# Two transformer blocks on one core: when the modulation, the norms' sums, the last mixer's meta queries and the store run

## What is computed

```python
for l in range(2):                                  # first block
    mod = silu(c) @ w_ada[l] + b_ada[l]             # and the same of c_ctx; w_ada[l] is 1024 x 6144
    sh1, sc1, gt1, sh2, sc2, gt2 = split(mod, 6)
    hx = rms_norm(x, g_norm1[l]) * (1 + sc1) + sh1  # the context tokens likewise
    q, k, v = split(hx @ w_in[l])                   # mixers a, b, c: attention, two with rope,
    o = concat(mixer_a, mixer_b, mixer_c)           # q and k normed by head; context for l = 0 only
    x = x + gt1 * (o @ w_out[l])
    hx2 = rms_norm(x, g_norm2[l]) * (1 + sc2) + sh2
    x = x + gt2 * conv_ffn(hx2, w_up[l], conv, w_down[l])
for l in range(2):                                  # second block, h = 16 meta tokens and x
    h = h + 0.5 * rmsnorm(swiglu(rmsnorm(h, g), w_ffn1_gu, w_ffn1_down), g)
    h = h + rmsnorm(token_mixer(rmsnorm(h, g)), g)  # forgetting attention (fox) and gated linear attention
    h = h + 0.5 * rmsnorm(swiglu(rmsnorm(h, g), w_ffn2_gu, w_ffn2_down), g)
return h[:, meta:]                                  # so the meta tokens' own rows of the last layer are not read
```

## Time and profile before

| what | value |
|---|---|
| median of 3 runs | 2582.66 us (2581.03 to 2585.74) |
| the profiled execution | 2583.32 us, span 2581.5 us |
| TensorE matmul busy | 2417.3 us, 94% |
| VectorE busy | 1478.6 us, 57% |
| ScalarE busy | 1210.6 us, 47% |
| GpSimd busy | 115.8 us, 4% |
| mean granted TensorE clock | 0.957 |
| transfers | 355.32 MB, mean 138 GB/s |
| chain that ended last | TensorE 82%, VectorE 8%, ScalarE 4%, issue 3%, DMA 2% |

### The profile page before, as it was taken

How to read it: one execution, slowest core, us unless ns; L and a number is a source line. 1 busy time by engine, 2 the same in 40 slices (tenths; PEclk the granted TensorE clock), 3 DMA queues, 4 the chain that set the end, 5 groups by cost and what they waited for, 6 DMA issues and landing times.

```text
span 2581.5 us, 48676 instructions
## 1 busy us (share of the span) xinstructions
PE 2417.3 (94%) x18241; PEld 2168.0 (84%) x18241; DVE 1478.6 (57%) x2455; ACT 1210.6 (47%) x2095; POOL 115.8 (4%) x196
## 2 busy tenths in 40 slices
PE   6799997999999799899999999999999998999998
PEld 4578675777777587899999988989999997898998
DVE  2354645555532555687566575566656647656664
ACT  1264733333322646565444455554445445565553
POOL 0001410000000004000000000000000000000000
PEclk8599997999999899899999989999999998999999
DMA  7721022545433230355555532435555553344554
GB/s 278 242 87 58 2 84 77 160 158 162 154 98 101 79 99 1 116 178 174 168 188 169 159 114 96 143 131 188 170 162 171 170 172 117 107 136 145 187 185 122
DMA packets 100475, 355.32 MB, mean 138 GB/s; under 512 B 11136, under 2 KB 12832, under 8 KB 100352
## 3 DMA queue, kind: packets, MB, share of 16 engines
q1 hardware_dynamic: 91264, 321.23, 38.6%
q0 software_dynamic: 9088, 32.41, 4.1%
HBM read 352.55 MB, written 1.05 MB: 137 GB/s over the span
## 4 chain that ended last, share of the span: by engine, by line
PE 82%; DVE 8%; ACT 4%; issue 3%; DMA 2%; DVEq 0%; ACTq 0%; POOL 0%; SPq 0%; POOLq 0%
PE ps L668 22%; PE ps L669 22%; PE ps L670 22%; PE ps L805 2%; DMA ada_raw<-in_w_ada 2%; DVE wl L1603 2%; PE ps L818 2%; ACT wh L1160 2%; PE ps L791 2%; PE ps L731 1%; PE ps L685 1%; PE ps L689 1%; PE ps L686 1%; DVE nrstd L1622 1%; DVE nh L1679 1%
## 5 line engine op out<-in xcount | busy, mean ns | idle before, releaser
L1603 DVE TENSOR_TENSOR wl<-raw,wh 128x1024 fp32r<-128x1024 f32 x574 | 701.3, 1223 | 560.9 <-ACT wh L1160 557.4
L668 PE MATMUL ps<-hH,wh 128*128 128x272 f32 (+2 forms) x2960 | 936.5, 316 | 45.0 <-DVE hL L1688 21.1
L669 PE MATMUL ps<-hL,wh 128*128 128x272 f32 (+2 forms) x2960 | 914.5, 309 | 0.0
L670 PE MATMUL ps<-hH,wl 128*128 128x272 f32 (+2 forms) x2960 | 912.7, 308 | 0.0
L1160 ACT ACTIVATE wh<-raw 128x1024 fp32r<-128x1024 f32 x574 | 602.1, 1052 | 371.3 <-PE ps L670 347.0
L668 PEld LDWEIGHTS ps<-hH,wh 128*128 128x128 f32 x2960 | 565.8, 191 | 93.6 <-issue 38.8
L670 PEld LDWEIGHTS ps<-hH,wl 128*128 128x128 f32 x2960 | 565.8, 191 | 24.0
L669 PEld LDWEIGHTS ps<-hL,wh 128*128 128x128 f32 x2960 | 566.5, 191 | 22.3 <-issue 1.7
L668 PE MATMUL ps<-actH,wh 128*128 128x272 f32 (+2 forms) x1136 | 344.1, 303 | 2.6 <-DVE wl L1603 2.1
L670 PE MATMUL ps<-actH,wl 128*128 128x272 f32 (+2 forms) x1136 | 343.5, 302 | 0.0
L669 PE MATMUL ps<-actL,wh 128*128 128x272 f32 (+2 forms) x1136 | 342.9, 302 | 0.0
(11 more groups left out here) (293 smaller groups left out, 2852.0 us busy)
## 6 DMA issues: line engine op xcount, KB each, us to landing
raw<-in_w_ffn_gu SPq DMA_DIRECT2D x176, 512.0 KB, 3.5
raw<-in_w_mix SPq DMA_DIRECT2D x98, 512.0 KB, 3.5
raw<-in_w_up SPq DMA_DIRECT2D x88, 512.0 KB, 3.5
raw<-in_w_ffn_down SPq DMA_DIRECT2D x64, 512.0 KB, 3.6
ada_raw<-in_w_ada SPq DMA_DIRECT2D x48, 512.0 KB, 5.2
ada_next<-in_w_ada POOLq DMA_DIRECT2D x48, 512.0 KB, 4.0
raw<-in_w_out SPq DMA_DIRECT2D x32, 512.0 KB, 3.4
raw<-in_w_down SPq DMA_DIRECT2D x32, 512.0 KB, 3.5
```

The lines of the kernel that those rows point to most:

```text
L668: pe.matmul(out, a_h, b_h, start=start, stop=False)
L669: pe.matmul(out, a_h, b_l, start=False, stop=False)
L670: return pe.matmul(out, a_l, b_h, start=False, stop=stop)
L1603: dve.tensor_tensor(wl[:, slot, :], raw[:, slot, :], wh[:, slot, :].bitcast(F32), ALU.subtract).then_inc(l_split, 1)
```

## The change

It does these things.

- Layer 0's modulation is made in two parts. Chunks 0 to 15 (`ADA_FIRST`, shift and scale of the first norm) come in the opening, with the first three weight chunks (`EARLY`) loaded between chunks 11 and 12, and the norm's sum after chunk 11. Chunks 16 to 47 are loaded by GpSimd's queue through two slots and multiplied two at a time between the head and value tiles (`rest_ada`, 16 places), their rows copied by VectorE (`rest_rows`) into one buffer, with `mod` of these made just before the attention.
- The tables are loaded once 12 chunks are used, not after the norm.
- The four norms use squares in a ring of two and a running sum (`sq_added`), made in the stage before (`in_out`, `in_down`), a last square summed by TensorE itself, Ln and Exp as root, and `first_group` for the first three tiles. Of the heads' sums and rotations, those of the first tiles are made later (`SUMS`, `TURNS`).
- Layer 1's modulation has seven chunks in the output projection instead of four.
- The lambda terms of both layers are made once, in the opening.
- The last mixer has 8 attention steps, without the meta queries.
- The last norm works on pairs of tiles, and each pair is stored by a transfer of its own.

```diff
@@ SyncE
+            for j in range(ADA_FIRST):
+                if j >= ADA_RING:
+                    sp.wait_ge(ada_used, j - ADA_RING + 1)
+                if j == ADA_FIRST - 4:
+                    for c in range(EARLY):
+                        sp.wait_ge(l_split, c + 1)
+                        sp.dma_start(raw[:, c, :], io["w_qk"][0, KT + c]).then_inc(raw_loaded[c], 16)
+                sp.dma_start(ada_raw[:, j % ADA_RING, :], io["w_ada"][0, j]).then_inc(ada_loaded[j % ADA_RING], 16)
...
-            sp.wait_ge(x_ready, 4 * 8 + 6)
-            sp.dma_start(io["out"].rearrange("(k p) t -> p k t", p=P), xT[:, :, X0:T1]).then_inc(out_done, 16)
-            sp.wait_ge(out_done, 16)
+            for q in range(4):
+                sp.wait_ge(last_pair, q + 1)
+                sp.dma_start(out[:, 2 * q:2 * q + 2], xT[:, 2 * q:2 * q + 2, X0:T1]).then_inc(out_done, 16)
@@ GpSimd
-                pool.wait_ge(h_ready, 8 * (2 * l + 1))
+                if l == 0:
+                    pool.wait_ge(ada_used, ADA_FIRST - 4)
...
+                if l == 0:
+                    for j in range(ADA_FIRST, NADA):
+                        pool.wait_ge(ada_used, j - 3 if j < ADA_FIRST + 2 else j - 1)
+                        pool.dma_start(ada_raw[:, j % 2, :], io["w_ada"][0, j]).then_inc(ada_rest_loaded[j % 2], 16)
@@ TensorE
             def norm(n):
-                pe.wait_ge(sum_ready, n.idx + 1)
-                pe.matmul(ps[:, 5, 0:n.T], ones[:], n.nrstd[:, 0, 0:n.T], start=True, stop=True).then_inc(ss_ready, 1)
+                pe.wait_ge(sq_added, (KT - 2) * (n.idx + 1))
+                pe.matmul(ps[:, 5, 0:n.T], ones[:], n.nrstd[:, 0, 0:n.T], start=True, stop=False)
+                pe.wait_ge(sq_ready, 8 * n.idx + 8)
+                pe.matmul(ps[:, 5, 0:n.T], ones[:], n.nsq[:, 1, 0:n.T], start=False, stop=True).then_inc(ss_ready, 1)
...
+                def rest_ada(h):
...
+                    g = (ADA_FIRST + 2 * h) // 4
+                    if h % 2 == 0:
+                        pe.wait_ge(ada_row_ready, g)
+                        if h:
+                            turn_rows(7, g - 1, ada_rows)
+                    for j in ada_hook(h):
+                        pe.wait_ge(ada_rest_loaded[j % 2], 16 * (h + 1))
+                        ada_chunk(6, j % 4, ada_raw[:, j % 2, :], silu_first)
...
+                first_group(S[f"k{l}"], hh_ready, h_ready, 8 * split_before[n.idx], T=T1)
+                rest_ada(0)
+                for i in range(GROUP, N_HEADT):
...
+                    head_sums(SUMS[i][0])
+                    rest_ada(i - 2)
...
-                feature_major(S[f"up{l}"], tq, n=n, after=None if l else next_ada)
+                first_group(S[f"up{l}"], hh_ready, h_ready, 8 * split_before[n.idx], T=tq)
+                feature_major(S[f"up{l}"], tq, after=None if l else next_ada, skip=GROUP)
@@ ScalarE
-            def norm(n):
...
+            def square(n, k):
+                if k >= 2:
+                    act.wait_ge(sq_added, (KT - 2) * n.idx + max(1, k - 2))
+                act.activation(n.nsq[:, k % 2, 0:n.T], xT[:, k, T1 - n.T:T1], ACT.Square, scale=D ** -0.5).then_inc(sq_ready, 1)
@@ VectorE
             def norm(n, before_scale=None):
-                while summed.get(n.idx, 0) < KT - 1:
-                    add_square(n)
-                dve.wait_ge(root_ready, n.idx + 1)
-                link(dve.reciprocal(n.rstd, n.rstd))
                 if before_scale:
                     before_scale()
+                dve.wait_ge(root_ready, n.idx + 1)
@@ mixer
-                self.i, self.g, self.p, self.qt = i, FOX_STEPS * l + i, i // 3, i % 3
+                self.i, self.g, self.p, self.qt = i, 12 * l + i, i // FOX_PER[l], i % FOX_PER[l] + l
@@ end
-            transition(norms["post_ffn2", 1])
+            last_norm(norms["post_ffn2", 1])
```

More of the change, by code:

```diff
@@ L304, in build_program @@
         ada_loaded = [sem(f"ada_loaded{s}") for s in range(ADA_RING)]
+        ada_rest_loaded = [sem(f"ada_rest_loaded{s}") for s in range(2)]
         ada_next_loaded = sem("ada_next_loaded")
@@ L846, in _ @@
             last.then_inc(cols_psum, 1)
+            pe.wait_ge(lam_prod, 1)
             for l in range(2):
-                pe.wait_ge(lam_prod, l + 1)
-                pe.matmul(ps[:, 6, 0:2], ones[:], lam[:, 0:2], start=True, stop=True).then_inc(lam_sum, 1)
+                last = pe.matmul(ps[:, 6, 2 * l:2 * l + 2], ones[:], lam[:, l, 0:2], start=True, stop=True)
+            last.then_inc(lam_sum, 1)
+            for l in range(2):
                 tq = T1 if l == 0 else TX
@@ new lines, in rest_rows, with first_modulation @@
+                def rest_rows(h):
+                    if l == 0 and h % 2:
+                        ada_rows_of((ADA_FIRST + 2 * h) // 4, 6)
+                def first_modulation():
+                    modulation(0, ADA_FIRST if l == 0 else NADA, ADA_FIRST // 4 if l == 0 else ADA_GROUPS)
+                if l == 0:
+                    n = norms["n1", 0]
+                    dve.wait_ge(tables_loaded, 16)
+                    link(dve.tensor_reduce(ada_sel[:], ident[:].rearrange("p (j c) -> p c j", c=32)[:, 0:2, :], AX.X, ALU.add))
+                    ada_rows_of(0, 0)
+                    for _ in range(KT - 2):
+                        add_square(n)
+                    ada_rows_of(1, 1)
+                    ada_rows_of(2, 0)
+                    for c in range(AHEAD):
+                        split(Stage("", None, 0, 0, 0, 0), Step(0, c, RING), 0)
+                    ada_rows_of(3, 1)
@@ L2041, in _ @@
+                norm(norms["n1", l], before_scale=first_modulation)
                 tiles = head_tiles(l)
```

367 lines of the change are left out of this document (217 added, 150 removed).

## The result

The changed kernel takes 2514.64 us (median of 4 runs, 2513.44 to 2526.68) beside 2581.85 for the kernel before: a ratio of 0.975, 95% interval 0.9717 to 0.9783. The forecast was 2504 with a range of 2492 to 2522. The time is in the range, 10.6 above the forecast; the gain is 67 us and not 79. The profiled execution took 2513.86 us, its span is 2511.8; the one of before 2583.32 and 2581.5.

The account below looks back on a forecast made before the run. The prediction took the opening to be bound by transfers (48 w_ada chunks, 25 MB) and the body by TensorE. Its terms summed to -78.9 us from the profiled 2583.3, by the median 2503.8: 2504 us, range 2492 to 2522.

Parts of the forecast that it names:

- Opening to the norm: Opening: 16 instead of 48 w_ada chunks ahead of the norm, which starts at 50.6 instead of 101.74: -51.1 us.
- Three tiles run together: Layer 0's first projections: norm start to end of third tile takes 19.8 us instead of 32.3, TensorE setting the pace: -12.5.
- w_ada in the projections: Layer 0's projections: 32 chunks at 0.57 and 8 turns at 0.92 on TensorE, +25.6 us; small load waits +2.
- the 11.7 from which they decide: Rival, layer 0's projections: POOL's loads land at their worst, 12.9 us; +98, 2602 us; decides from about 11.7; chance 0.03.
- Catch-up: Layers 0 and 1: late square sums delay ScalarE, which in layer 1 must catch up: +2 and +3 us.
- n2 of layer 0: Norm before layer 0's up stage: third tile at 427.5 instead of 446.4: -18.9 us, 9.9 of it the start.
- n1 of layer 1: Norm before layer 1's heads: third tile at 863.0 instead of 878.5, less 0.46 for a head's sums: -15.0 us.
- n2 of layer 1: Norm before layer 1's up stage, 256 columns: third tile at 1075.8 instead of 1083.5: -7.8 us.
- Attention openings: Opening of each attention: a low half and a split leave VectorE's path: -1.2 us.
- Mixer: Mixer of layer 1: four meta-query steps go, each 0.26 for scores, 0.1 transposes, 0.22 values: -2.3 us.
- End: End: eight steps of 512 columns -0.35, and only the last 256 KB stored behind the last add, 2.3 less: -2.7 us.
- half restarts: Rival: restarts give half, ones-matmuls and first tiles at low clock, h's pace holding the group: +17, about 2521; chance 0.09.

Follow-up runs that it names:

- experiment 1: The changed kernel run again unedited, as yardstick on the same chip: 2519.45 us, ratio 0.9761 to the kernel before.
- experiment 10: Changed kernel with the head and bias tables issued when 16 w_ada chunks are used instead of 12: 2509.56 us, ratio 0.973 to the kernel before.
- experiment 4: Changed kernel with layer 1's head tiles run one by one instead of the first three together: 2516.44 us, ratio 0.9742 to the kernel before.
- experiment 3: Changed kernel with layer 1's up tiles run one by one instead of the first three together: 2516.59 us, ratio 0.9734 to the kernel before.
- experiment 5: Changed kernel with the four meta-query steps back in layer 1's mixer (12 steps, not 8): 2520.28 us, ratio 0.9752 to the kernel before.
- experiment 11: Changed kernel with one 1 MB store behind the last pair instead of four of 256 KB: 2523.16 us, ratio 0.9771 to the kernel before.
- experiment 6: Changed kernel with layer 0's head tiles run one by one instead of the first three together: 2519.91 us, ratio 0.9758 to the kernel before.
- experiment 7: Changed kernel with layer 0's up tiles run one by one instead of the first three together: 2515.62 us, ratio 0.9757 to the kernel before.
- experiment 8: Changed kernel with square root and reciprocal in the first block's four norms instead of Ln and Exp: 2530.27 us, ratio 0.9809 to the kernel before.

## Why the prediction came out right, and 10 us too good

Added up along the kernel by TensorE's own rows: at the end of layer 0's down stage it is 51.9 us ahead, where the terms make 53.5; at the end of layer 1's output stage 55.5, where they make 66.1; at the end 69.7 against 78.9. So most of what is missing arises in layer 1's heads and attention. Of that, the step of the prediction that failed is the catch-up behind the group, taken at 3 and measured at 6.2; the attention's part is chance. The row copy in layer 0's up stage cost 5.5, for which the sum had nothing, and was made good by an early opening and cheaper w_ada. All this is one trace: by experiment 1's medians (2519.45, still in the range) the forecast is 15 too good.

- **Opening to the norm: -51.1 forecast, -53.7 in the trace.** Held up: bytes at the measured rate set it (experiment 10). This execution was among the early ones: over the ten with this opening the norm starts at 50.2 in the mean, where the forecast had 50.6, and they spread over 5 us, for which it had no term.
- **"Three tiles run together": -12.5.** The 19.8 us from the norm to the third tile came out to the tenth in this trace; that is luck in part, since the other kernels with this group show 19.8 to 21.4. The reason was wrong. Without the group 4.7 of the 12.5 are lost. The rest goes with the norm's new order and the weight splits made ahead of it, read from the rows (first matmul 2.0 us behind the norm's start instead of 13.9) and tested by no run. After the catch-up, 0.2 to 3.4 us are the group's.
- **w_ada in the projections: +25.6, and +2 for loads.** Measured: pairs at 1.01 and turns at 0.88, 16 and 8 of them, 23.2, with no wait for a load at any of the 16 places; a chunk is 0.505 us and not the 0.57 of the earlier trace rows. The loads land in 4.5 us at the median, and but for the first pair, which has 34 us, 6.3 at most, far from the 11.7 from which they decide. The rule of the Trainium skill that was weighed there (SBUF — State Buffer, "SBUF: two separate sides") had no effect that these rows show; but no row tells whether VectorE ran anything in a two-port mode beside these loads, so it is not tested, here or in the earlier trace rows.
- **Catch-up: +2 and +3.** Layer 0: 1.84. Layer 1: this is the term that was mis-sized. The waits for sums and rotations are 9.0 us against 2.8 before, so 6.2, and 5.1 without the group (experiment 4). It was inside the bounds of 10 that the text gave, and taken at 3 although the text named the four heads and four copies that ScalarE has to make good.
- **n2 of layer 0: -18.9.** The start and the third tile came as forecast (18.3 by the tile behind the group). Then the row copy cost 5.5, so that the stage has -12.8. The text counted "a late copy of rows" (the 1.98 us at 429.19 above) among what this restart would get rid of, and gave no reason why the copy would come sooner. Behind a group VectorE has four evictions and a split to do at once, and TensorE waits for the copy that is queued behind them: 3.38 us and the low clock. "VectorE's idle half", by which the text calls other copies hidden, those of layer 0's late rows, is an average; these did stay hidden but for 0.8 us.
- **n1 of layer 1: -15.0.** To the third tile: 39.6 us before, 24.4 after, -15.3. Right, and then the catch-up took half: the heads went from 97.0 to 90.7.
- **n2 of layer 1: -7.8.** -9.2 at the third tile, but the stage ends with -4.9: the lead melts at 0.1 us a tile (experiment 3).
- **Attention openings: -1.2.** From the last value matmul to the first score it takes 2.8 us instead of 3.4 in layer 0, although the last w_ada pair and a turn now lie in it, and 2.55 instead of 3.2 in layer 1: -1.2, and the same within 0.03 us in the repeat. What lies behind is longer in this trace, from first score to output stage by 1.0 us in layer 0 and 2.8 in layer 1. In the other kernels, with the same code, it is 0.2 shorter to 1.5 longer and 0.2 shorter to 2.8 longer than before, so this part of the missing 10 us is chance.
- **Mixer: -2.3.** 1.04 a step, 4.2 in all (experiment 5). Its pieces were too low, 0.3 against 0.22 a step for the values, 0.2 against 0.1 for the transposes, 0.4 against 0.26 for the scores, and the wait that the text let stay went with them in part. The window of the earlier trace rows holds the values of three steps and the text divided by four (the row of the whole stage stands in experiment 5).
- **End: -2.7.** 2.9 in the trace, 2.2 of it the four stores (experiment 11), between the 2.3 of bytes alone and the 1.8 that the text estimated from "Anatomy of one DMA" (DMA: Bandwidth & Descriptors, the Trainium skill). The fit there is of transfers issued from GpSimd, while SyncE issues this store. Another 3 us of this trace's lead, in the last up stage, are no part of the change (last section). That the four pay their fixed part one after the other is excluded.

Of the rivals, "half restarts" (2521) came nearer to the measured time than the forecast, with the wrong cause: the restarts did not fail, what follows them gave back. The largest surprise is what the groups are worth. By experiments 6, 4, 7 and 3, in this order, the group of layer 0's heads gains 0.2 to 3.4 us, that of layer 1's heads loses 1.2 to 4.3, that of layer 0's up stage loses 1.5 to 3.5 (with its row copy moved ahead it would gain 3.5 to 4), and that of layer 1's up stage does nothing within 1 us: in sum nothing or a small loss, although each brings its third tile 3.5 to 5.6 us earlier. The restarts' gain comes from Ln and Exp (10.6, experiment 8) and, by the rows of before and after only, from squares, sums and weight splits made ahead; no run takes these back, so their share is not shown.

## What to carry to other kernels

A stop that is shortened by running several tiles together hands its work to the engines behind in one lump: before counting its gain, list what is queued behind that lump on each engine and who waits for it (a copy of rows, a late sum), and move the small one that is waited for ahead. Price such a rearrangement at the end of its stage and not at its third tile. In an opening that is bound by bytes, everything that is issued ahead of the last needed chunk and used later belongs behind it.

## What the runs showed of the hardware that was not expected

- **TensorE runs at two spacings while its granted clock reads full.** 40 us in the last up stage, the same code in the kernel after and in that of experiment 3, without a wait:

```profile
2385.00:2425.00 40.00, 40.00 (x355) 40.00 (x354) 28.64 (x47) 21.00 (x31) 0.00 (x0) 1.00 0.64 199
```

```profile
2385.00:2425.00 40.00, 40.00 (x342) 40.00 (x341) 27.30 (x43) 19.14 (x28) 0.00 (x0) 1.00 0.60 189
```

355 matmuls against 342, both at 1.00. Four tiles (96 matmuls) take 10.88 us in the one and 11.31 in the other, throughout. Three of the 13 profiled executions of changed kernels take 128.6 to 128.7 us for this stage, ten 131.1 to 132.2. The kernel after happened to be among the three, so that some 3 us of its gain at the end (-2.9 in this stage against before) are no part of the change. What chooses the spacing is open.

- **The opening's transfers spread by 5 us** between executions of the same opening (norm at 47.7 to 52.5), as much as or more than five of the sum's eleven terms.
- **A repeated pass of small matmuls is cheaper than the first**: 0.435 us a chunk against 0.505, so a price from doubling is a lower bound.
